# Zeros of the gate cells stored during attention, and twelve modulation dot products computed under the output projection

## The chip, the cores and the metric

One core of one Trainium2 chip runs the whole kernel. The metric is the device time of one execution in microseconds (us), as the median of three. The engines are TensorE (PE in the profile), VectorE (DVE), ScalarE (ACT), GpSimd (POOL) and SyncE (SP), which here only issues DMAs.

## What is computed

A decoder layer on x (512 tokens x 1024) with a conditioning vector c, all in float32:

```
mod = silu(c) @ w_mod + b_mod            # six parts of 1024: shift_m scale_m gate_m shift_f scale_f gate_f
h = rms_norm(x, pre_mix_gain) * (1 + scale_m) + shift_m
y = hybrid_mixer(h)                      # differential attention and gated DeltaNet heads, then y @ w_out
x = x + gate_m * rms_norm(y, post_mix_gain)
h = rms_norm(x, pre_ffn_gain) * (1 + scale_f) + shift_f
y = peer_ffn(h)                          # 8 heads pick 16 of 128^2 experts per token
x = x + gate_f * rms_norm(y, post_ffn_gain)
```

The peer stage doesn't gather expert rows for 384 of the 512 tokens. It multiplies by all experts in 128 tiles and needs a dense array of gate weights in DRAM (`gate_scratch`, 128 x 128 x 384 cells), nearly all zero, into which the picked gates are scattered.

## The kernel before, in words

Each engine's program is written out by hand; semaphores order them, and each engine and each DMA queue works strictly in its own order. Every float32 weight tile (128x1024, 512 KB) is split in two for PE: ACT casts it to `whi`, and DVE or POOL subtracts to get the remainder `wlo`; PE then does three products. Tiles are numbered through the kernel: 0 to 7 (values, z), 8 to 15 (keys and queries of attention), 16 to 27 (DeltaNet's q, k, v), 28 to 35 (`w_out`), 36 to 51 (query), 52 on (experts). Four raw buffers take them from DRAM; `load_raw(n, ...)` on SP waits for remainder n-4.

**Modulation.** `mod` is taken as 48 column tiles of 128x1024, each reduced on DVE against silu(c) in `gate_f` by one instruction, `mod_tile(m)` (L1756, both operands in SBUF), which then counts up `s_modu`. Tiles 0 to 15 give shift_m and scale_m, 16 to 23 gate_m, 24 to 39 shift_f and scale_f, 40 to 47 gate_f (much later). `mod_columns` (L1763 to L1766) turns the sums into the columns `acol` and `bcol`, a few tiny instructions; those of the second half are first used when the second norm is applied, after the output projection (L816 on ACT, L2176 on DVE). SP loads the tiles: of 16 to 39 four before each of the weight tiles 8 to 13. `EARLY` is 32: tiles 24 to 31 run on DVE ahead of attention, 32 to 39 two at a time in its first four steps, with `mod_columns` in the fourth.

**Attention** is run in 18 steps (s = 0 to 17), step s sharing its time with weight tile 10+s on PE: PE multiplies that tile, then does `scores(s)` (L1272), `transposes(s-1)` (L1281) and `values(s-2)` (L1298). ACT casts tile 12+s and takes exponentials, POOL makes the remainders (`lo`, L624), DVE does `biased` (L1891), the modulation tiles, the convolutions from step 6 on and `difference` (L1901 to L1906), on which PE's transposes wait. After it come the decay rows and their exponent in `E` (the buffer `vbeta`), then some 55 us of inverting triangular blocks, and the scan over four chunks (to 307).

**Zeros.** POOL fills `zeros` (8 KB per partition, over attention's keys) after the last scores, L642, and SP stores it 24 times, 1 MB each (L518), after the loads of tiles 28 to 31 and before those of 32 to 35. POOL waits for them (`s_zst`) before it scatters the first gates.

**Output projection** (PE, 307 to 354): tiles 28 to 31 into banks 0 to 3 for all four token blocks (`out_tile`, L1579 to L1581), with `head_transposes` 4 to 7 (L1535) between the first of them, then tiles 32 to 35 block by block into banks 4 to 7 (L1599 to L1601). Around it: ACT casts tiles 30 to 35 (`out_hi`, L1020) and rounds the transposed heads (`o_rounded`, L998); DVE makes their remainders (`o_remainder`, L2101: one operand in PSUM); each `out_tile` waits for two. POOL makes the weight remainders of tiles 30 to 35 (L670), then those of query tiles 36 and 37 (L675). When the first four banks are done, ACT squares them (L1030) and DVE multiplies them by the gate (`y_by_gate`, L2144, the bank is in PSUM). Then per block b: ACT squares the second half, DVE `block_mean` (L2132, L2134), a root on ACT, DVE adds into `xn` (L2166), ACT squares that (L1062) and scales it (L1041). PE transposes the scaled blocks (L1612, L1619), with short dummy products between them (`WARM_QUERY`, L1615), and starts the query projection (L1635) once the norm's columns have been applied.

SP's order here: the loads of tiles 28 to 31, the 24 stores, tiles 32 to 35, x again (four loads, after the heads are normed), query tiles 36 to 39, then the stores of x1.

Of the kernel before, what the change touches and what calls it, by code (L numbers as in the profile page):

```python
# [35 lines left out]
P = 128  # L36
# [46 lines left out]
FIRST_PACED, LAST_PACED = 7, 124  # L83
POOL_DOWN = 9
LAST = 2
EARLY = 32
GDN_ORDER = (4, 5, 6, 7, 0, 1, 2, 3, 8, 9, 10, 11)
WARM = 11
WARM_QUERY = 6
# [10 lines left out]
def build(nc, x, c, mod_tiles, mod_bias_col, gain_cols, in_tiles,  # L100
# [6 lines left out]
    with ExitStack() as ctx:  # L107
# [87 lines left out]
        QKT = at("QKT", [P, NB, 512], F32)  # L195
        wT = at("wT", [P, NB, 512], F32)
        egT = at("egT", [P, NB, 512], F32, cursor[0] - NB * 512 * 4)
        carried = vbeta[:, 0, :]
        E = vbeta
        v_copy = {10: state, 11: vnew}  # L200
# [74 lines left out]
        qTs = at("qTs", [P, 2, SEQ], F32)  # L275
        hfl2 = at("hfl2", [P, 4, SEQ], F32)
        modf = at("modf", [P, 8, D], F32, phase + 32 * 1024)
        zeros = at("zeros", [P, NB * SEQ], F32, kq)
        cursor[0] = phase + 64 * 1024
        whi4 = at("whi4", [P, WSLOT, D], F32R)  # L280
        wlo4 = at("wlo4", [P, WSLOT, D], F32R)
# [178 lines left out]
        def mod_slot(m):  # L460

            if m < 16:
                t = modr[:, m % 8, :]
            elif m < 40:
                t = modx[:, m % 4, :] if m % 8 < 4 else modr[:, m % 4, :]
            else:
                t = modf[:, m % 8, :]
            return t, s_modl[m % 8], 16 * (m // 8 + 1)
# [8 lines left out]
        def _(sp):  # L477
# [7 lines left out]
            def load_mod(m):  # L485
                if m == 16:
                    sp.wait_ge(s_xT, KD)
                if 8 <= m < 40:
                    sp.wait_ge(s_modu, m - 7)
                dst, landed, _ = mod_slot(m)  # L490
                dq(dst, mod_tiles[m]).then_inc(landed, 16)

# [10 lines left out]
            for dst, src in [(mrow[:, 0:48], conv_col),  # L503
                             (hgain, head_gain_cols),
                             (alog4, a_log.partition_broadcast(P)),
                             (dt4, dt_bias.partition_broadcast(P)),
                             (lam_in, lambdas.partition_broadcast(P))]:
                dq(dst, src).then_inc(s_hc, 16)
            for n in range(T_KQ, T_OUT):
                for m in range(4 * n - 16, min(4 * n - 12, 40)):  # L510
                    load_mod(m)
                load_raw(n, in_tiles[n if n < T_GDN else T_GDN + GDN_ORDER[n - T_GDN]])
            for n in range(4):
                load_raw(T_OUT + n, out_tiles[n])
            gate_cells = gate_flat[0:CELLS].rearrange("(p q) -> p q", p=P)
            sp.wait_ge(s_zm, 1)
            for q in range(TD * P // (NB * SEQ)):
                dq(gate_cells[:, q * NB * SEQ:(q + 1) * NB * SEQ], zeros[:]).then_inc(s_zst, 16)  # L518
            for n in range(4, 8):
                load_raw(T_OUT + n, out_tiles[n])  # L520

            sp.wait_ge(s_on, NB)
            for b in range(NB):
                dq(xn[:, b, :], x[b]).then_inc(s_xr, 16)
            for n in range(4):
                load_raw(T_QUERY + n, query_tiles[n])
            for b in range(NB):
# [75 lines left out]
        def _(pool):  # L603
# [33 lines left out]
            lo(T_KQ + 1, T_KQ + 1)  # L637
            pool.wait_ge(s_lo, SLOT0 + 1)
            lo(SLOT0 + 1, SLOT0 + 1)
            lows(SLOT0 + 2, T_OUT)  # L640
            pool.wait_ge(s_sc, H * NB)
            g.memset(zeros[:], 0.0).then_inc(s_zm, 1)  # L642

            for n in range(4 * NB):
                k, t = divmod(n, NB)
# [21 lines left out]
            for n in range(T_OUT + 2, T_QUERY):  # L667
# [2 lines left out]
                g.tensor_tensor(l[:], raw[:, n % RAW, :].rearrange("p (a n) -> p a n", a=2),  # L670
                                h[:].bitcast(F32), ALU.subtract).then_inc(s_lo, 1)

            for n in range(2):
                pool.wait_ge(s_hi, T_QUERY + n + 1)
                g.tensor_tensor(wlo4[:, 2 + n, :], raw[:, (T_QUERY + n) % RAW, :],  # L675
                                whi4[:, 2 + n, :].bitcast(F32), ALU.subtract).then_inc(s_lo, 1)
# [9 lines left out]
            expert_rows = expert_tiles.rearrange("n p d -> (n p) d")  # L686

            gate_cells = gate_flat.unsqueeze(1)
            pool.wait_ge(s_zst, 16 * TD * P // (NB * SEQ))
            for b in range(NG):  # L690
                for k in range(PICKS):
                    if k % MGROUP == 0:
# [42 lines left out]
        def _(act):  # L735
# [135 lines left out]
            for s in range(T_OUT - SLOT0):  # L871
                if s < H * NB:
                    hi(SLOT0 + s + 2)
                if SLOT0 + s < T_GDN:
                    kq_copy(SLOT0 + s)
                if s == H * NB:
                    act.wait_ge(s_oa, SUMS_AT + 1)
                    sc.activation(k_sums, k_sums, ACT.Ln, bias=eps_t).then_inc(s_l2r, 1)
                    act.wait_ge(s_l2, 1)
                    sc.activation(q_sums, bank[2][:, 0:16], ACT.Ln, bias=eps_t).then_inc(s_l2r, 1)  # L880
                if s < H * NB:
                    exps(s)
                if 1 <= s <= H * NB:
                    copy_t(s - 1)
                if s == H * NB:
                    act.wait_ge(s_used, T_OUT - 1)
                    sc.copy(v_copy[10][:], bank[T_OUT % 2][:]).then_inc(s_vc, 1)
                    hi(T_OUT)
                if s in (10, 14):
                    g = (s - 10) // 4  # L890
                    c0 = GDN_ORDER[4 * g]
                    act.wait_ge(s_conv, 4 * g + 4)
                    sc.activation(qkvT[:, c0:c0 + 4, :], qkvT[:, c0:c0 + 4, :],
                                  ACT.Silu).then_inc(s_silu, 1)
                    if g == 0:
                        act.wait_ge(s_modu, 40)
                if s in (11, 14):
                    g = (s - 11) // 3
                    c0 = GDN_ORDER[4 * g]
                    act.wait_ge(s_silu, g + 1)  # L900
                    for n in range(c0, c0 + 4):
                        sc.activation(l2r[:, n, :], qkvT[:, n, :], ACT.Square).then_inc(s_sq, 1)
# [816 lines left out]
        def _(dve):  # L1719
# [127 lines left out]
            dve.wait_ge(s_baT, 1)  # L1847
            v.tensor_copy(baT[:], bank[2][0:8, :]).then_inc(s_bac, 1)
            for m in range(24, EARLY):
                if m == 29:  # L1850
                    dve.wait_ge(s_lo, SLOT0)
                    weight_low(SLOT0)
                mod_tile(m)
            dve.wait_ge(s_lame, 1)
            tt(lam[:, 2:3], lam[:, 0:1], lam[:, 1:2], ALU.subtract)
            v.drain()
# [83 lines left out]
            for s in range(T_OUT - SLOT0):  # L1940
                if 3 <= s <= H * NB + 1:
                    attn_out(s - 3)
                if s < H * NB:
                    biased(s)
                if s == H * NB:
                    k_columns()
                for m in range(EARLY + 2 * s, min(EARLY + 2 * s + 2, 40)):
                    mod_tile(m)
                if EARLY + 2 * s == 38:
                    mod_columns(1, 0, KD)  # L1950
                if T_GDN <= SLOT0 + s < T_OUT - 2:
                    conv(SLOT0 + s - T_GDN)
                if s < H * NB:
                    difference(s)

            for t in range(NB):
                dve.wait_ge(s_row, t + 1)
                decay_args(E, t, ROW_BANK[t], M_NOT_AFTER).then_inc(s_du[0], 1)
# [163 lines left out]
            mean_squares(NB - 1)  # L2123
            gated_heads(NB - 1)
            normed_heads(NB - 1)
            for k in range(4, KD):
                o_remainder(k)

            def block_mean(b):  # L2130
# [362 lines left out]
```

## Time and profile before

| | |
|---|---|
| median of three runs | 1694.61 us (1694.39 to 1695.78) |
| the profiled execution | 1693.73 us |
| its span, first to last instruction | 1691.9 us |
| PE busy | 1675.7 us, 99% |
| DVE busy | 1200.0 us, 71% |
| ACT busy | 691.0 us, 41% |
| POOL busy | 910.8 us, 54% |
| mean granted TensorE clock | 0.998 |
| modulation tiles 0 to 39 on DVE (L1756) | 57.5 us in 40 instructions |

All starts are counted in us from the first instruction. "Busy" of PE is modelled from pipelined matmuls and says little by itself; what counts is where PE has idle time in front of an instruction, which a timeline gives in brackets with the engine that ended it.
### The profile page before, as it was taken

Reading aid. Unit: us, or ns where it says so; the run is one execution under the profiler, and the core shown is the slowest. Engines: PE = TensorE matmul, PEld = TensorE weight load, DVE = VectorE, ACT = ScalarE, POOL = GpSimd, SP = SyncE. Lnnn points to the kernel's source line nnn. Section 1 sums busy time; section 2 is a strip of 40 time slices with the busy share of each in tenths; the row PEclk is TensorE's granted clock in tenths of the full one; section 3 lists DMA queues with packets and bytes.
Section 4 is the critical chain, followed back from the end, with each engine's and each line's share of the span. In section 5 each row is a group of like instructions: output and inputs, shape, how many; then the busy total and the mean of one; then the engine's idle time right before and its main releaser. Section 6 shows DMA issues by size and latency. Waiting matters only on the chain.

```text
span 1691.9 us, 25803 instructions
## 1 busy us (share of the span) xinstructions
PE 1675.7 (99%) x8018; PEld 1389.1 (82%) x8018; DVE 1200.0 (71%) x2991; ACT 691.0 (41%) x1049; POOL 910.8 (54%) x730
## 2 busy tenths in 40 slices
PE   9999999999999999999999999999999999999998
PEld 7777888878888888888888888888888888888886
DVE  8877576446697887777777732224888888888886
ACT  6445564553342244444344434423333333333333
POOL 0133213413357666667666776664676776777630
PEclk9999999999999999999999999999999999999999
DMA  9932393332246444444444444449999999999994
GB/s 372 334 121 72 126 417 133 122 127 75 88 143 241 142 147 150 143 143 143 149 140 141 149 149 149 138 142 351 332 367 378 342 390 350 374 373 349 390 337 154
DMA packets 149221, 375.69 MB, mean 222 GB/s; under 512 B 32033, under 2 KB 64929, under 8 KB 145954
## 3 DMA queue, kind: packets, MB, share of 16 engines
q1 hardware_dynamic: 114338, 307.52, 50.8%
q0 software_dynamic: 34816, 67.41, 11.1%
q8 instruction: 25, 0.41, 0.1%
q14 instruction: 42, 0.34, 0.1%
HBM read 311.73 MB, written 63.11 MB: 222 GB/s over the span
## 4 chain that ended last, share of the span: by engine, by line
PE 95%; DVE 2%; DMA 1%; ACT 1%; DVEq 0%; SPq 0%; issue 0%; ACTq 0%
PE bank L1184 17%; PE bank L1185 17%; PE bank L1186 17%; PE bank L1684 10%; PE bank L1686 10%; PE bank L1688 10%; PE bank L1445 1%; PE bank L1629 1%; DMA g_in<-gate_scratch 1%; PE bank L1272 1%; PE bank L1427 1%; PE bank L1298 1%; PE bank L1461 1%; PE bank L1226 0%; PE bank L1581 0%; PE bank L1601 0%
## 5 line engine op out<-in xcount | busy, mean ns | idle before, releaser
L701 POOL DMA_INDIRECT gate_scratch<-merged,idx_cell x384 | 429.9, 1120 | 213.8 <-issue 106.6
L1184 PE MATMUL bank<-act_hi,whi 128*128 128x512 f32 x1296 | 508.3, 392 | 0.0
L1186 PE MATMUL bank<-act_hi,wlo 128*128 128x512 f32 x1296 | 505.1, 390 | 0.0
L1185 PE MATMUL bank<-act_lo,whi 128*128 128x512 f32 x1296 | 505.1, 390 | 0.0
L2189 DVE TENSOR_TENSOR wlo<-raw,whi 128x1024 fp32r<-128x1024 f32 x247 | 302.0, 1223 | 225.5 <-ACT whi L1092 224.0
L1684 PE MATMUL bank<-whi,chi 128*128 128x512 f32 x768 | 298.8, 389 | 0.7 <-DVE clo L2366 0.7
L1686 PE MATMUL bank<-wlo,chi 128*128 128x512 f32 x768 | 298.8, 389 | 0.0
L1688 PE MATMUL bank<-whi,clo 128*128 128x512 f32 x768 | 298.8, 389 | 0.0
L1186 PEld LDWEIGHTS bank<-act_hi,wlo 128*128 128x128 f32 x1296 | 243.6, 188 | 50.9
L1184 PEld LDWEIGHTS bank<-act_hi,whi 128*128 128x128 f32 x1296 | 243.8, 188 | 49.7
L1185 PEld LDWEIGHTS bank<-act_lo,whi 128*128 128x128 f32 x1296 | 243.8, 188 | 49.4
L1098 ACT ACTIVATE aout<-bank 128x512 f32<-128x512 f32 x128 | 76.6, 599 | 370.2 <-PE bank L1186 357.7
L719 POOL DMA_INDIRECT rows<-in_expert_tiles,idx_row x128 | 171.4, 1339 | 104.5 <-DVE ysp L2381 78.9
L624 POOL TENSOR_TENSOR wlo<-raw,whi 128x1024 fp32r<-128x1024 f32 x35 | 84.9, 2429 | 232.2 <-ACT whi L748 232.2
L1129 ACT CAST chi<-coef 128x384 fp32r<-128x384 f32 x128 | 65.6, 513 | 323.0 <-PE bank L1688 179.2
L710 POOL DMA_INDIRECT asp<-act_scratch,idx_act x128 | 160.9, 1257 | 56.4 <-issue 38.4
L2381 DVE SCALAR_TENSOR_TENSOR ysp<-rows,csp,ysp 128x1024 f32<-128x1024 f32 x127 | 163.2, 1285 | 12.1 <-issue 0.4
L1684 PEld LDWEIGHTS bank<-whi,chi 128*128 128x128 f32 x768 | 144.2, 188 | 31.0 <-issue 1.1
L1688 PEld LDWEIGHTS bank<-whi,clo 128*128 128x128 f32 x768 | 144.2, 188 | 29.8
L1686 PEld LDWEIGHTS bank<-wlo,chi 128*128 128x128 f32 x768 | 144.2, 188 | 29.8
L1092 ACT CAST whi<-raw 128x1024 fp32r<-128x1024 f32 x128 | 133.4, 1042 | 1.0 <-DMA raw<-in_expert_tiles 0.7
L1143 ACT CAST whi<-raw 128x1024 fp32r<-128x1024 f32 x125 | 131.2, 1049 | 0.0
(392 smaller groups left out, 1840.5 us busy)
## 6 DMA issues: line engine op xcount, KB each, us to landing
raw<-in_expert_tiles SPq DMA_DIRECT2D x256, 512.0 KB
act_scratch<-aout SPq DMA_DIRECT2D x128, 256.0 KB, 2.1
gate_scratch<-zeros SPq DMA_DIRECT2D x24, 1024.0 KB, 22.2
a_in<-act_scratch SPq DMA_DIRECT2D x128, 192.0 KB, 7.0
g_in<-gate_scratch SPq DMA_DIRECT2D x128, 192.0 KB
modr<-in_mod_tiles SPq DMA_DIRECT2D x28, 512.0 KB, 10.7
raw<-in_in_tiles SPq DMA_DIRECT2D x28, 512.0 KB
raw<-in_query_tiles SPq DMA_DIRECT2D x16, 512.0 KB
```

The source lines that it names most:

```text
L701: g.indirect_dma_start(out=gate_cells, out_offset=bass.IndirectOffsetOnAxis(ap=idx_cell[:, b, k:k + 1], axis=0), in_=merged[:, b, k:k + 1] ...
L710: g.indirect_dma_start(out=asp[:, k:k + 1], out_offset=None, in_=act_cells, in_offset=bass.IndirectOffsetOnAxis(ap=idx_act[:, k:k + 1], ax ...
L719: g.indirect_dma_start(out=rows[:, k % ROWS, :], out_offset=None, in_=expert_rows, in_offset=bass.IndirectOffsetOnAxis(ap=idx_row[:, k:k + ...
L1092: sc.copy(whi4[:, n % WSLOT, :], raw[:, n % RAW, :]).then_inc(s_hi, 1)
L1184: mm(out_bank[:], whi[:, slot, w], act_hi[:, k, :], start=(k == 0), stop=False)
L1185: mm(out_bank[:], whi[:, slot, w], act_lo[:, k, :], start=False, stop=False)
L1186: last = mm(out_bank[:], wlo[:, slot, w], act_hi[:, k, :], start=False, stop=(k == KD - 1))
L1684: mm(o, chi[:, j % WSLOT, a], whi4[:, j % WSLOT, w], start=start, stop=False, skip_group_check=True)
L1686: mm(o, chi[:, j % WSLOT, a], wlo4[:, j % WSLOT, w], start=False, stop=False, skip_group_check=True)
L1688: return mm(o, clo[:, j % WSLOT, a], whi4[:, j % WSLOT, w], start=False, stop=stop, skip_group_check=True)
L2189: tt(wlo4[:, n % WSLOT, :], raw[:, n % RAW, :], whi4[:, n % WSLOT, :].bitcast(F32), ALU.subtract).then_inc(s_lo, 1)
L2381: stt(out=ysp[:], in0=rows[:, k % ROWS, :], scalar=c, in1=ysp[:], op0=ALU.mult, op1=ALU.add).then_inc(s_axpy, 1)
```

## The change

`EARLY` goes from 32 to 28: modulation tiles 24 to 27 stay ahead of attention, none runs in it, and 28 to 39 with `mod_columns` run on DVE after the heads are normed, between and behind o remainders 4 to 7. Their buffers are six slots of 128x1024 in `Tm`, `PM` and `va`, which are free then; SP loads six of them after the u/w products (`s_uw`), between out tiles 33 and 34, and the other six after x, ahead of the query tiles, each when the tile six before it is used. POOL waits for tile 35 (`s_modu` 36) before it writes the remainders of the query tiles, which lie over `Tm`.

`zeros` becomes the buffer `vbeta`, filled by POOL between the remainders of weight tiles 11 and 12. SP stores it twice after each of the loads of weight tiles 13 to 24. DVE waits for all 24 before it writes `E` there.

```diff
-EARLY = 32
+EARLY = 28
+FILLS = 24
+FILL_FROM = 13
+LATE_SLOTS = 6
...
+        zeros = vbeta
+        late_mods = [ap[:, a:a + 2, :].rearrange("p a n -> p (a n)")
+                     for ap in (Tm, PM, va) for a in (0, 2)]
...
-        zeros = at("zeros", [P, NB * SEQ], F32, kq)
...
+            elif m < EARLY:
+                t = modx[:, m % 4, :] if m % 8 < 4 else modr[:, m % 4, :]
             elif m < 40:
-                t = modx[:, m % 4, :] if m % 8 < 4 else modr[:, m % 4, :]
+                t = late_mods[(m - EARLY) % LATE_SLOTS]
...
-                if 8 <= m < 40:
+                if 8 <= m < EARLY:
                     sp.wait_ge(s_modu, m - 7)
+                elif EARLY + LATE_SLOTS <= m < 40:
+                    sp.wait_ge(s_modu, m - LATE_SLOTS + 1)
...
             for n in range(T_KQ, T_OUT):
-                for m in range(4 * n - 16, min(4 * n - 12, 40)):
+                for m in range(4 * n - 16, min(4 * n - 12, EARLY)):
                     load_mod(m)
                 load_raw(n, in_tiles[n if n < T_GDN else T_GDN + GDN_ORDER[n - T_GDN]])
+                if n == FILL_FROM:
+                    sp.wait_ge(s_zm, 1)
+                for q in range(max(2 * (n - FILL_FROM), 0), min(2 * (n - FILL_FROM) + 2, FILLS)):
+                    dq(gate_cells[:, q * NB * SEQ:(q + 1) * NB * SEQ],
+                       zeros[:].rearrange("p t n -> p (t n)")).then_inc(s_zst, 16)
             for n in range(4):
                 load_raw(T_OUT + n, out_tiles[n])
-            gate_cells = gate_flat[0:CELLS].rearrange("(p q) -> p q", p=P)
-            sp.wait_ge(s_zm, 1)
-            for q in range(TD * P // (NB * SEQ)):
-                dq(gate_cells[:, q * NB * SEQ:(q + 1) * NB * SEQ], zeros[:]).then_inc(s_zst, 16)
-            for n in range(4, 8):
-                load_raw(T_OUT + n, out_tiles[n])
+            load_raw(T_OUT + 4, out_tiles[4])
+            load_raw(T_OUT + 5, out_tiles[5])
+            sp.wait_ge(s_uw, NB)
+            for m in range(EARLY, EARLY + LATE_SLOTS):
+                load_mod(m)
+            load_raw(T_OUT + 6, out_tiles[6])
+            load_raw(T_OUT + 7, out_tiles[7])
 
             sp.wait_ge(s_on, NB)
             for b in range(NB):
                 dq(xn[:, b, :], x[b]).then_inc(s_xr, 16)
+            for m in range(EARLY + LATE_SLOTS, 40):
+                load_mod(m)
...
             pool.wait_ge(s_lo, SLOT0 + 1)
             lo(SLOT0 + 1, SLOT0 + 1)
+            pool.wait_ge(s_baT, 1)
+            g.memset(zeros[:], 0.0).then_inc(s_zm, 1)
             lows(SLOT0 + 2, T_OUT)
-            pool.wait_ge(s_sc, H * NB)
-            g.memset(zeros[:], 0.0).then_inc(s_zm, 1)
...
+            pool.wait_ge(s_modu, EARLY + LATE_SLOTS + 2)
             for n in range(2):
                 pool.wait_ge(s_hi, T_QUERY + n + 1)
...
-                        act.wait_ge(s_modu, 40)
+                        act.wait_ge(s_modu, EARLY)
...
             for m in range(24, EARLY):
-                if m == 29:
-                    dve.wait_ge(s_lo, SLOT0)
-                    weight_low(SLOT0)
                 mod_tile(m)
+            dve.wait_ge(s_lo, SLOT0)
+            weight_low(SLOT0)
...
-                for m in range(EARLY + 2 * s, min(EARLY + 2 * s + 2, 40)):
-                    mod_tile(m)
-                if EARLY + 2 * s == 38:
-                    mod_columns(1, 0, KD)
...
+            dve.wait_ge(s_zst, 16 * FILLS)
             for t in range(NB):
                 dve.wait_ge(s_row, t + 1)
                 decay_args(E, t, ROW_BANK[t], M_NOT_AFTER).then_inc(s_du[0], 1)
...
-            for k in range(4, KD):
-                o_remainder(k)
+            mod_tile(28)
+            o_remainder(4)
+            o_remainder(5)
+            for m in range(29, 32):
+                mod_tile(m)
+            o_remainder(6)
+            o_remainder(7)
+            for m in range(32, 40):
+                mod_tile(m)
+            mod_columns(1, 0, KD)
```

## Rows read from the trace of the kernel before

**Rows 1.** The page, part 4: the chain that ended last, by engine.

```profile
PE 95%; DVE 2%; DMA 1%; ACT 1%; DVEq 0%; SPq 0%; issue 0%; ACTq 0%
```

**Rows 2.** Waits of PE, whole run: us in total, times, longest us.

```profile
PE bank L1281 <- DVE pr L1906: 0.8, 2, 0.7
```

**Rows 3.** Timeline of PE, second attention step: start us, us, engine line op out<-in [idle before].

```profile
92.94 0.33 PE L1281 MATMUL bank<-ident,pr 128*128 128x128 f32 x1 [0.68 <-DVE pr L1906]
```

**Rows 4.** Timeline of DVE, modulation tiles before and in attention.

```profile
59.24 3.42 DVE L1756 CUSTOM_DVE_ANT_0 modr<-modr,gate_f 128x1024 f32<-128x1024 f32 x1
...
87.98 2.80 DVE L1756 CUSTOM_DVE_ANT_0 modx<-modx,gate_f 128x1024 f32<-128x1024 f32 x1
...
90.71 1.22 DVE L1756 CUSTOM_DVE_ANT_0 modx<-modx,gate_f 128x1024 f32<-128x1024 f32 x1
```

**Rows 5.** Timeline of DVE, output projection to the last block's mean.

```profile
315.41 0.75 DVE L2101 SCALAR_TENSOR_TENSOR act_lo<-bank,mrow,act_lo 128x512 fp32r<-128x512 f32 x1 [2.12 <-ACT act_lo L998]
...
321.76 0.75 DVE L2101 SCALAR_TENSOR_TENSOR act_lo<-bank,mrow,act_lo 128x512 fp32r<-128x512 f32 x1 [4.08 <-ACT act_lo L998]
...
334.11 2.48 DVE L2144 TENSOR_TENSOR xs<-bank,gate_m 128x512 f32<-128x512 f32 x4 [10.08 <-ACT osq L1030]
338.62 0.62 DVE L2132 TENSOR_TENSOR small<-small 128x1 f32<-128x1 f32 x1 [2.02 <-ACT osq L1030]
...
354.87 0.16 DVE L2132 TENSOR_TENSOR small<-small 128x1 f32<-128x1 f32 x1 [1.59 <-ACT osq L1030]
```

**Rows 6.** Timeline of POOL, output projection.

```profile
313.10 2.43 POOL L670 TENSOR_TENSOR wlo_x<-raw,whi_x 128x1024 fp32r<-128x1024 f32 x1 [11.42 <-ACT whi_x L1020]
...
322.74 2.40 POOL L670 TENSOR_TENSOR wlo<-raw,whi 128x1024 fp32r<-128x1024 f32 x1 [2.49 <-ACT whi L1020]
328.13 2.39 POOL L670 TENSOR_TENSOR wlo_x<-raw,whi_x 128x1024 fp32r<-128x1024 f32 x1 [2.99 <-ACT whi_x L1020]
333.57 2.42 POOL L670 TENSOR_TENSOR wlo_y<-raw,whi_y 128x1024 fp32r<-128x1024 f32 x1 [3.05 <-ACT whi_y L1020]
336.83 4.75 POOL L675 TENSOR_TENSOR wlo<-raw,whi 128x1024 fp32r<-128x1024 f32 x2 [0.85 <-ACT whi L741]
```

**Rows 7.** Timeline of ACT, output projection.

```profile
327.00 1.05 ACT L1020 CAST whi_x<-raw 128x1024 fp32r<-128x1024 f32 x1 [3.75 <-PE bank L1581]
...
343.75 0.58 ACT L1030 ACTIVATE osq<-bank 128x512 f32<-128x512 f32 x1
...
348.71 0.60 ACT L1030 ACTIVATE osq<-bank 128x512 f32<-128x512 f32 x1 [0.59 <-PE bank L1601]
```

**Rows 8.** Timeline of POOL, before and in attention's first steps.

```profile
58.95 2.63 POOL L624 TENSOR_TENSOR wlo<-raw,whi 128x1024 fp32r<-128x1024 f32 x1 [55.95 <-ACT whi L748]
...
80.78 2.40 POOL L624 TENSOR_TENSOR wlo<-raw,whi 128x1024 fp32r<-128x1024 f32 x1 [13.56 <-ACT whi L748]
86.97 2.73 POOL L624 TENSOR_TENSOR wlo<-raw,whi 128x1024 fp32r<-128x1024 f32 x1 [3.79 <-ACT whi L748]
```

**Rows 9.** The tile `zeros`: its stores and its memset.

```profile
L518 SPq DMA_DIRECT2D gate_scratch<-zeros x24: 343/1255/4209, 203.1 to 240.5; - x24
L642 POOL MEMSET zeros<- x1: 1809/1809/1809, 201.3 to 201.3; 128x2048 f32 x1
```

**Rows 10.** Timeline of ACT, the cast of weight tile 14.

```profile
98.86 1.05 ACT L748 CAST whi<-raw 128x1024 fp32r<-128x1024 f32 x1 [4.01 <-PE bank L1186]
```

**Rows 11.** Windows of ten us: us, busy by engine (instructions), PEclk, DMA share, GB/s.

```profile
250.00:260.00 10.00, 10.00 (x93) 8.68 (x91) 7.51 (x14) 4.27 (x10) 4.54 (x6) 1.00 1.01 416
...
270.00:280.00 10.00, 10.00 (x96) 8.62 (x94) 7.09 (x12) 3.68 (x8) 4.05 (x2) 1.00 0.32 107
```

**Rows 12.** Timeline of SP's queue, the first query tiles.

```profile
320.30 16.04 SPq L496 DMA_DIRECT2D raw<-in_query_tiles  x4
```

**Rows 13.** Windows of ten us, as rows 11.

```profile
190.00:200.00 10.00, 10.00 (x43) 7.51 (x43) 4.95 (x13) 8.53 (x13) 2.08 (x2) 0.83 0.16 54
...
350.00:360.00 10.00, 9.31 (x64) 8.17 (x62) 5.38 (x14) 5.85 (x12) 0.00 (x0) 1.00 0.27 107
```

More of the change, by code:

```diff
@@ L508, in _ @@
                 dq(dst, src).then_inc(s_hc, 16)
+            gate_cells = gate_flat[0:CELLS].rearrange("(p q) -> p q", p=P)
             for n in range(T_KQ, T_OUT):
-                for m in range(4 * n - 16, min(4 * n - 12, 40)):
+                for m in range(4 * n - 16, min(4 * n - 12, EARLY)):
                     load_mod(m)
                 load_raw(n, in_tiles[n if n < T_GDN else T_GDN + GDN_ORDER[n - T_GDN]])
+                if n == FILL_FROM:
[3 more added lines that the diff above has]
+                       zeros[:].rearrange("p t n -> p (t n)")).then_inc(s_zst, 16)
             for n in range(4):
                 load_raw(T_OUT + n, out_tiles[n])
-            gate_cells = gate_flat[0:CELLS].rearrange("(p q) -> p q", p=P)
-            sp.wait_ge(s_zm, 1)
-            for q in range(TD * P // (NB * SEQ)):
-                dq(gate_cells[:, q * NB * SEQ:(q + 1) * NB * SEQ], zeros[:]).then_inc(s_zst, 16)
-            for n in range(4, 8):
-                load_raw(T_OUT + n, out_tiles[n])
+            load_raw(T_OUT + 4, out_tiles[4])
[5 more added lines that the diff above has]
+            load_raw(T_OUT + 7, out_tiles[7])
             sp.wait_ge(s_on, NB)
@@ L688, in _ @@
             gate_cells = gate_flat.unsqueeze(1)
-            pool.wait_ge(s_zst, 16 * TD * P // (NB * SEQ))
+            pool.wait_ge(s_zst, 16 * FILLS)
             for b in range(NG):
```

## The prediction

> **What bounds the kernel now.** Read first the chain of work that ended last [rows 1]: 95% of the span is TensorE (PE) matmuls, so only what makes PE wait, or lets it start sooner, can move the time. Second, PE's own waits over the whole run [rows 2]: the only one that the attention stage's VectorE (DVE) work causes is 0.8 us in two pieces. PE's timeline shows the larger, 0.68 us, at 92.94 [rows 3]. Behind it stand two modulation tiles (32 and 33) on DVE, from 87.98 to about 91.9 [rows 4]. Third, the timelines of DVE, GpSimd (POOL) and ScalarE (ACT) in the output projection, from 307 to 355, where the change puts twelve such tiles [rows 5 to 7]. There PE has no gap at all until 354.1; DVE looks nearly free, 10 us idle before 334.11. What the reader is to see is that POOL is not free there, and that DVE and POOL do not run independently.
>
> **One rule read from the trace first.** A modulation tile reads two 128x1024 operands from SBUF. Alone it takes 1.22 us, 1.145 from one start to the next [rows 4]. The tile at 87.98 took 2.80, and POOL's weight remainder at 86.97 took 2.73, so ended at 89.70: the tile ended 1.08 after it [rows 4, 8]. At 59.24 the same: POOL's began at 58.95 while a tile ran, took 2.63 instead of 2.40, and the next tile, issued at 59.24, ended at 62.66, 1.08 after POOL's end. So they exclude each other: whoever waits gets its turn when the running instruction ends, although the other engine has its next one ready. The tiny DVE addition at 338.62 took 0.62 and so ended where the first of POOL's two back-to-back remainders did (336.83 + 2.4), so a held DVE instruction gets in between them [rows 5, 6]. DVE instructions with one operand in PSUM aren't held: the o remainder at 315.41 took 0.75 while POOL ran [rows 5, 6].
>
> The Trainium skill says this as a rule ("SBUF — State Buffer", section "Who interferes with whom"): a DVE instruction with two SBUF inputs and a GpSimd instruction that reads SBUF block each other for the whole instruction. It speaks against this change: by a plain sum of DVE durations the twelve tiles fit, by the rule they don't. The trace agrees with it, with the 2.80 and 3.42 us above.
>
> **Attention, costed.** Removed: tiles 28 to 31 before it (4 x 1.145 = 4.6 us of DVE, under PE's projection tiles, nothing on the path), tiles 32 to 39 and the column step in its first four steps (8 x 1.145 and four holds behind POOL). On the path that is worth PE's 0.8 us and no more, since PE has no other wait for DVE there [rows 2]. Gain 0.8.
>
> Added to the SP queue: 24 stores of zeros, two after each weight tile 13 to 24. Each loads the DMA engines for about 2.5 us (the 24 went out from 203.1 to 240.5 [rows 9] and kept them full to about 264). POOL's memset (1.81 us [rows 9]) now stands between remainders 11 and 12. The first starts at 80.78 and ends at 83.2, the second starts at 86.97 [rows 8], so the memset fits in that pause, to 85.0. SP waits for it with tiles 14 and on queued behind: tile 14 lands after two stores, about 92, tile 15 after four, about 99, tile 16 after six, about 105. ACT wants tile 14 at 98.86 [rows 10] and each next one about 7 us later, 105.8 and 113.2. So 6 us at least are left, and after that 2.5 MB per 7.2 us step is 350 GB/s against the 416 that these engines moved in full stretches [rows 11]. Cost 0; if stores ran at half that rate, PE would wait some 5 us there. DVE's wait for all 24 before the decay rows ends near 160, and those come at 209: 0. The stretch 203 to 264, now free of stores, gains nothing: PE issues 93 instructions in ten us with the DMA engines full and 96 with a third of them busy, in a different mix [rows 11]. ACT's wait for 28 tiles instead of 40 is long over: 0. The six early loads on SP wait for the u/w products (290) and are in by 300: 0.
>
> **Output projection, costed.** The lock has to serve, from 313.1: six weight remainders of 2.4 us (tiles 30 to 35), twelve tiles of 1.1 us and the small column step (0.65, a drain in it), and, if they are ready, the two query remainders (36, 37; 4.75 together) [rows 6]. Walking through it with turns alternating: remainder 30 313.1 to 315.5; tile 28 to 316.6; remainder 31 to 319.0; o remainders 4 and 5 on DVE meanwhile; tile 29 to 320.0; remainder 32 to 322.4; tile 30 to 323.5; remainder 33 to 325.9; tile 31 to 327.0. Only then o remainders 6 and 7, to 328.4 (before: from 321.76). PE's fourth tile wants them when the third ends at 326.9 (ACT's cast at 327.00 starts on that [rows 7]): PE waits 1.4. Remainder 34 to 330.5; tiles 32 to 35 to 335.05 (which also frees POOL's new wait); remainder 35 to 337.5, in time for PE's moved need at 337.9; tile 36 to 338.5; query remainder 36 to 340.9, tile 37 to 342.0, query remainder 37 to 344.4, tiles 38 and 39 and the column step to 347.3.
>
> Loads: tiles 34 to 39 wait for slots (tile m for m-6), the last at 332.8, and the four query tiles on SP are behind them, about 333 instead of 320.3 [rows 12]. ACT wants the first at 337: 0.
>
> Behind the tiles in DVE's order stand the four gate products (2.48 us, PSUM operands), which before began at 334.11 and left 2.0 of slack before the mean of block 0 at 338.62. That mean now comes at 349.8. From there each block takes 4.37 to 4.4 us through ACT and DVE (343.75 to 348.71 less the 0.59 waited for PE [rows 7]), so the mean of block 3 comes at 363.0 instead of 354.87 [rows 5]: 8.1 us. PE's 1.4 lies inside it, since PE's last block then ends at 355.5 and PE has to wait for this chain anyhow. From there to the query projection all is as before.
>
> **TensorE's clock.** PE will have some 16 us (355.5 to 371) with only transposes and short dummy multiplications. The granted clock in thin work: full from 350 to 360, where the present burst of that kind lies, but 0.83 from 190 to 200, that is 3.4 of the ten us at the lower level (1.2 GHz), after 3 us of 128x1 products [rows 13]. Bounds: 0, and 1.7 us (3.4 us at half pace). The new gaps between bursts are about 3 us, nearest to the second, so I take 1.7.
>
> **Sum.** -0.8 + 8.1 + 1.7 = +9.0. The profiled execution took 1693.7 (span 1691.9), which gives 1702.7; the median of the runs is 0.9 higher, 1694.6, so 1703.6.
>
> **Rivals.**
> 1. Forecast, 0.62: the lock fills the output projection. 1701.9 without the clock's drop, 1703.6 with it, 1705.2 if waiting DVE loses to POOL's back-to-back remainders (the same walk then puts block 3's mean 9.7 late).
> 2. Partly, 0.18: the query remainders come after the tiles (ACT's casts late, or POOL's turn lost). The tiles then end at 342.5, the mean of block 3 is 3.3 late, and the run ends at 1697.1, or 1698.8 with the clock. It decides if both query remainders begin after 342.
> 3. No lock to speak of, 0.13: the tiles take 12 x 1.145 + 2.8 of o remainders + 0.65 from 313.3, so end at 330.5, ahead of the gate products. 1693.8, and 1692.1 if the clock's dip at 191 goes too. For it: DVE's 10 us of idle time. Against it: six held tiles in the trace, none that ran through a POOL remainder.
> 4. Faster, over 0.2%, 0.05: PE's steps in the inversion or attention were slowed by stores or by DVE work in a way that its waits don't show. Against it [rows 2, 11].
> 5. The zeros delay weight tiles 14 to 16 in attention, 0.02: +5 on top of any of these.
>
> No-change is within 0.2% (3.4 us, about what a measurement of this kernel can tell): rival 3 and the lower part of rival 2 lie in it. So slower 0.8, same 0.15, faster 0.05. The range, 1696.5 to 1707, leaves out rivals 3 and 4 and takes in the bounds of the clock and of the lock's order.
>
> **What would show it.** In the profile after: tiles of L1756 between 313 and 347 with durations near 2.2 to 3.5 us where POOL's remainders run, and a sum well over 14; POOL remainders of more than 2.4; PE's wait for DVE before the fourth out tile near 1.4; the first gate product near 347, and PE idle some 8 us more between 355 and 372; no wait at 92.9; no raw tile late in 85 to 160. Wrong, if the tiles' mean stays at 1.2 or if the gate products still begin by 337.

## The result, and the profile after

The change made the kernel **slower by 0.31%**: median 1699.23 us of eight runs (1698.40 to 1700.79) against 1694.5 of eight runs of the kernel before on the same chip; ratio 1.0031, 95% interval 1.0020 to 1.0042. The profiled execution took 1700.06 us, 6.4 more than that of before, with a span of 1698.3 against 1691.9. The forecast was 1703.6, in a range of 1696.5 to 1707.0. So the medians moved by 4.7 us where 9.1 was forecast.

PE's waits after the change, whole run (us in total, times, longest us; beside [rows 2]):

```profile
PE bank L1631 <- DVE xn L2189: 3.0, 1, 3.0
PE bank L1631 <- ACT xs L1060: 1.6, 1, 1.6
...
PE bank L1598 <- DVE act_lo L2116: 1.2, 1, 1.2
...
PE bank L1618 <- POOL wlo_y L688: 0.3, 1, 0.3
```

Three of the four lines are new, the second was 0.2 before; the wait for `pr` in attention (0.8) is gone. L1631 is PE's transposes ahead of the query projection, L1598 the fourth out tile, L1618 the out tiles of the second half. So PE now stands still just where DVE carries the moved tiles, and behind them. The chain that ended last says the same in shares (beside [rows 1]):

```profile
PE 93%; DVE 4%; issue 1%; DMA 1%; ACT 1%; DVEq 0%; SPq 0%; POOL 0%; POOLq 0%; ACTq 0%
```

DVE's timeline from the last head's norm to block 3's mean (beside [rows 5]; L1775 is the modulation tile, 28 to 39 in order, L2116 the o remainder, L2167 the gate product, L2155 the block mean):

```profile
311.88 0.17 DVE L2109 RECIPROCAL gsm<-gsm 128x4 f32<-128x4 f32 x1
...
312.74 3.41 DVE L1775 CUSTOM_DVE_ANT_0 Tm<-Tm,gate_f 128x1024 f32<-128x1024 f32 x1
...
316.08 1.40 DVE L2116 SCALAR_TENSOR_TENSOR act_lo<-bank,mrow,act_lo 128x512 fp32r<-128x512 f32 x2
317.40 2.10 DVE L1775 CUSTOM_DVE_ANT_0 Tm<-Tm,gate_f 128x1024 f32<-128x1024 f32 x1
...
319.43 3.40 DVE L1775 CUSTOM_DVE_ANT_0 PM<-PM,gate_f 128x1024 f32<-128x1024 f32 x1
...
327.42 1.21 DVE L1775 CUSTOM_DVE_ANT_0 va<-va,gate_f 128x1024 f32<-128x1024 f32 x1
...
345.93 2.48 DVE L2167 TENSOR_TENSOR xs<-bank,gate_m 128x512 f32<-128x512 f32 x4
348.32 0.15 DVE L2155 TENSOR_TENSOR small<-small 128x1 f32<-128x1 f32 x1
...
361.05 0.16 DVE L2155 TENSOR_TENSOR small<-small 128x1 f32<-128x1 f32 x1 [0.42 <-ACT osq L1049]
```

Beside it POOL's timeline (beside [rows 6]):

```profile
312.63 2.43 POOL L688 TENSOR_TENSOR wlo_x<-raw,whi_x 128x1024 fp32r<-128x1024 f32 x1 [11.42 <-ACT whi_x L1039]
315.03 3.38 POOL L688 TENSOR_TENSOR wlo_y<-raw,whi_y 128x1024 fp32r<-128x1024 f32 x1
...
338.49 5.84 POOL L694 TENSOR_TENSOR wlo<-raw,whi 128x1024 fp32r<-128x1024 f32 x2 [0.84 <-ACT whi L760]
```

Read the first lines of the two together. POOL's remainder runs from 312.63 to about 315.0; the tile, issued at 312.74, ends at 316.15, 1.1 later. POOL's next remainder was issued at 315.03 and takes 3.38: about 1.0 in which the tile still ran, and its own 2.4. Then a tile, then POOL, in turn. The groups of L1775 between 310 and 347 sum it up (busy us, mean ns):

```profile
L1775 DVE CUSTOM_DVE_ANT_0 va<-va,gate_f 128x1024 f32<-128x1024 f32 x4 | 11.3, 2857 | 0.0
L1775 DVE CUSTOM_DVE_ANT_0 PM<-PM,gate_f 128x1024 f32<-128x1024 f32 x4 | 11.3, 2855 | 0.0
L1775 DVE CUSTOM_DVE_ANT_0 Tm<-Tm,gate_f 128x1024 f32<-128x1024 f32 x4 | 7.9, 1982 | 0.0
```

That is 30.5 us for twelve tiles that need 1.14 to 1.22 each: eight were held. DVE, which before idled 10 us ahead of its gate products, now has no idle time there, and the gate products begin at 345.93 instead of 334.11.

**A ruler for the stage.** Executions differ in where this stage begins (309.63 us in e9 to 312.78 in e1, and 318.58 in e6), so I measure the stage inside each execution: from DVE's last `gsm` reciprocal (all heads normed) to PE's first product of the query projection. Before the change, DVE's and PE's timelines:

```profile
312.35 0.17 DVE L2094 RECIPROCAL gsm<-gsm 128x4 f32<-128x4 f32 x1
```

```profile
362.72 0.47 PE L1635 MATMUL bank<-act_hi,whi 128*128 128x512 f32 x1 [1.25 <-DVE act_lo L1778]
```

and after it, on PE:

```profile
327.64 0.47 PE L1598 MATMUL bank<-whi_y,act_lo 128*128 128x512 f32 x1 [1.20 <-DVE act_lo L2116]
...
368.91 0.47 PE L1654 MATMUL bank<-act_hi,whi 128*128 128x512 f32 x1 [1.25 <-DVE act_lo L1797]
```

362.72 - 312.35 = 50.37 before and 368.91 - 311.88 = 57.03 after: the stage is **6.66 us longer**, which is all that was lost: the span grew by 6.4, since the stage began 0.47 earlier, and what follows it took 0.2 longer. By the same ruler, every kernel of the experiments below, one profiled execution of each:

| kernel | stage, us | over before |
|---|---|---|
| before | 50.37 | 0 |
| after | 57.03 | +6.66 |
| e1 zeros only | 50.38 | +0.01 |
| e2 tiles only | 56.83 | +6.46 |
| e3 query remainders after the tiles | 56.91 | +6.54 |
| e4 no SBUF reads on POOL | 50.41 | +0.04 |
| e5 spread in attention | 50.37 | 0.00 |
| e6 the same, with the zeros | 50.39 | +0.02 |
| e7 query remainders after the columns | 53.86 | +3.49 |
| e8 eight late tiles | 50.39 | +0.02 |
| e9 query remainders twice | 61.26 | +10.89 |

Ten-us windows after the change (columns as in [rows 11], beside [rows 13]):

```profile
190.00:200.00 10.00, 10.00 (x43) 7.39 (x42) 5.00 (x14) 8.49 (x12) 2.05 (x2) 0.83 0.17 54
350.00:360.00 10.00, 7.04 (x38) 5.77 (x37) 5.68 (x15) 7.04 (x15) 0.00 (x0) 1.00 0.27 107
360.00:370.00 10.00, 6.43 (x49) 5.36 (x47) 5.80 (x14) 7.18 (x16) 0.00 (x0) 1.00 0.26 105
```

PE is down to 7.04 and 6.43 busy us in ten, and the granted clock stays at full speed: the clock costs nothing. The dip at 190 is as it was in this execution, but it doesn't belong to the kernel. The window of e3, whose code is that of the change up to the output projection:

```profile
190.00:200.00 10.00, 10.00 (x53) 7.80 (x53) 6.49 (x16) 9.91 (x16) 3.21 (x2) 1.00 0.18 54
```

**How the time ahead of the stage divides.** Counted from PE's first weight product (near 19 to 20 us) to the stage's beginning, before and e1 take 293.10 and 293.07 us, the change 292.09, and e2, e3, e4, e5, e7, e8 and e9 all 290.48 to 290.50. The first three have the dip at 190 (0.83 in its window), the seven have not (1.00). So with the dip on both sides the removal of attention's wait is worth 1.0 us, and an execution without the dip is another 1.6 shorter. The change's own profile shows that its absence isn't assured by the new order; how often it comes, one profile per kernel can't tell.

### The profile page after: what moved, and what is told of

Its sections match the earlier page's. It is cut to its first block, busy times and chain, and to the rows that moved or that the text cites. A ratio compares the mean times of both kernels' runs of the same rounds, so it can differ in the third digit from the quotient of the medians.

```text
span 1698.3 us, 25805 instructions
## 1 busy us (share of the span) xinstructions
PE 1677.3 (99%) x8018; PEld 1389.8 (82%) x8018; DVE 1207.3 (71%) x2991; ACT 689.7 (41%) x1049; POOL 919.1 (54%) x730
## 4 chain that ended last, share of the span: by engine, by line
PE 93%; DVE 4%; issue 1%; DMA 1%; ACT 1%; DVEq 0%; SPq 0%; POOL 0%; POOLq 0%; ACTq 0%
PE bank L1203 17%; PE bank L1204 17%; PE bank L1205 17%; PE bank L1703 10%; PE bank L1705 10%; PE bank L1707 10%; PE bank L1464 1%; PE bank L1648 1%; DMA g_in<-gate_scratch 1%; PE bank L1291 1%; DVE va L1775 1%; DVE PM L1775 1%; PE bank L1446 1%; PE bank L1317 1%; PE bank L1480 1%
```

## The experiments

e1 to e4 and e5 to e8 are two sets, each with its own runs of the kernel before, and e9 is a third by itself, so ratios compare across sets and medians only within one. The medians of before are 1692.68, 1694.29 and 1693.01.

### The two halves apart (e1, e2)

e1 is the kernel before with the zeros' part of the diff alone: tiles 32 to 39, their loads and the column step stay as before. Its edit to the kernel before:

```diff
+        zeros = vbeta
...
-        zeros = at("zeros", [P, NB * SEQ], F32, kq)
...
+                if n == FILL_FROM:
+                    sp.wait_ge(s_zm, 1)
+                for q in range(max(2 * (n - FILL_FROM), 0), min(2 * (n - FILL_FROM) + 2, FILLS)):
...
+            dve.wait_ge(s_zst, 16 * FILLS)
```

e2 is the change with the zeros, their memset and the 24 stores put back where they were. Its edit to the change:

```diff
-        zeros = vbeta
+        zeros = at("zeros", [P, NB * SEQ], F32, kq)
...
-                if n == FILL_FROM:
-                    sp.wait_ge(s_zm, 1)
...
+            sp.wait_ge(s_zm, 1)
+            for q in range(FILLS):
+                dq(gate_cells[:, q * NB * SEQ:(q + 1) * NB * SEQ], zeros[:]).then_inc(s_zst, 16)
...
```

> Only the zeros part of the change; the modulation tiles stay as before, in attention. Theory A (in the output projection DVE's twelve tiles and POOL's weight remainders take turns at one lock, and that alone makes the change slower): as before, ratio 1.000 within 0.001, PE's 0.8 us wait at attention's second step still there, no new wait. Theory B (DVE's order is simply too full there, lock or not): the same as A. Theory C (the stores or the changed loads on SP's queue cost the time): 4 to 6 us slower than before, with weight tiles that land late.

> Only the moved modulation tiles; the zeros are made and stored as before. Theories A and B: as slow as the whole change, ratio about 1.003 (4 to 6 us over before), the gate products start near 346 in the profile. Theory C: no slower than before.

e1: 1692.72 us, ratio 1.0000 (0.9991 to 1.0009). e2: 1698.31, ratio 1.0033 (1.0020 to 1.0045). PE's waits in e1 still hold the one of attention, and none for a raw tile or for what the stores could delay:

```profile
PE bank L1285 <- DVE pr L1910: 0.8, 2, 0.7
```

PE's waits in e2 are those of the change:

```profile
PE bank L1629 <- DVE xn L2186: 2.8, 1, 2.8
...
PE bank L1596 <- DVE act_lo L2113: 1.2, 1, 1.2
```

The zeros are free, and the twelve tiles carry the whole loss.

### POOL without reads (e4)

POOL's remainders of tiles 30 to 37 are replaced by two fills each, about as long together (2 x 0.95 us), which write the same buffers and read none. The third product of those tiles is thereby made with zeros: this kernel leaves out that part of the computation, though PE does as many products.

```diff
-                g.tensor_tensor(l[:], raw[:, n % RAW, :].rearrange("p (a n) -> p a n", a=2),
-                                h[:].bitcast(F32), ALU.subtract).then_inc(s_lo, 1)
+                g.memset(l[:].bitcast(F32), 0.0)
+                g.drain()
+                last = g.memset(l[:].bitcast(F32), 0.0)
+                last.then_inc(s_lo, 1)
...
```

> The changed kernel with POOL's remainders of out tiles 30 to 35 and query tiles 36 and 37 left out: instead POOL writes zeros to each of the eight buffers twice (1.8 us each, no operand read), so those tiles' third product is with zeros. POOL stays occupied for most of the time, but reads nothing. Theory A: every modulation tile takes 1.22 us, they end near 330, the gate products start at 333.6 when the banks are done, and the time falls by 6.6 us from the changed kernel's, to about 1 us under before. Theory B: 2 us at most, the tiles still end after the gate products' due time. Theory C: no change.

1691.68 us, ratio 0.9994 (0.9985 to 1.0003), stage +0.04. POOL's and DVE's timelines:

```profile
311.37 0.95 POOL L688 MEMSET wlo_x<- 128x1024 f32 x1 [11.41 <-ACT whi_x L1043]
312.45 0.95 POOL L690 MEMSET wlo_x<- 128x1024 f32 x1
```

```profile
311.49 1.22 DVE L1779 CUSTOM_DVE_ANT_0 Tm<-Tm,gate_f 128x1024 f32<-128x1024 f32 x1
...
326.94 1.23 DVE L1779 CUSTOM_DVE_ANT_0 Tm<-Tm,gate_f 128x1024 f32<-128x1024 f32 x1 [2.28 <-DMA Tm<-in_mod_tiles]
...
335.08 2.48 DVE L2171 TENSOR_TENSOR xs<-bank,gate_m 128x512 f32<-128x512 f32 x4
```

The tile at 311.49 runs beside a fill at its full pace. All twelve take 1.22 or 1.23, eight of them beside a fill. Now their loads set the pace (2.28 us of waiting for tile 34), and it no longer matters. This is the decisive run: the same twelve tiles, in the same place, cost nothing once POOL reads nothing. Not the number of tiles, not their loads, but the exclusion is the price. (A pair of fills is also 0.4 us shorter than the remainder in whose place it stands; the tiles beside a fill show that it isn't this.) The Trainium skill ("SBUF — State Buffer", section "Who interferes with whom") says that a DVE instruction with two SBUF inputs contends with a GpSimd instruction that reads SBUF and "not with one that only writes it"; the trace agrees, 3.41 against 1.22 us.

### The query remainders later (e3, e7) and twice (e9)

The walk put the last tiles and the column step behind POOL's query remainders 36 and 37. All three are edits to the change. e3 lets POOL wait for all 40 tiles first:

```diff
-            pool.wait_ge(s_modu, EARLY + LATE_SLOTS + 2)
+            pool.wait_ge(s_modu, 40)
```

e7 lets it wait for the column step as well:

```diff
-            pool.wait_ge(s_modu, EARLY + LATE_SLOTS + 2)
+            pool.wait_ge(s_cols, 6)
```

e9 makes each of the two remainders twice:

```diff
-                g.tensor_tensor(wlo4[:, 2 + n, :], raw[:, (T_QUERY + n) % RAW, :],
-                                whi4[:, 2 + n, :].bitcast(F32), ALU.subtract).then_inc(s_lo, 1)
+                for again in range(2):
+                    last = g.tensor_tensor(wlo4[:, 2 + n, :], raw[:, (T_QUERY + n) % RAW, :],
+                                           whi4[:, 2 + n, :].bitcast(F32), ALU.subtract)
+                    if again == 0:
+                        g.drain()
+                last.then_inc(s_lo, 1)
```

> The changed kernel, but POOL waits for all 40 modulation tiles, not for 36, before its two remainders of query tiles 36 and 37. Neither has work added or removed. Theory A: the lock is free for the last tiles, so they end 4.7 us earlier, the mean of block 3 comes near 356.3 instead of 361.05 in the profile, and the time falls by 4 to 4.8 us, to about that of before (1694.5). The query remainders then run from about 341 to 346, long before PE needs them. Theory B: DVE's own work is as long as ever, so no change, 1699. Theory C: no change.

> The changed kernel, but POOL waits for the column step that follows modulation tile 39 before its two query remainders. In the run where it waited for the 40 tiles alone, the two remainders began at 339.77 and held the column step's tiny additions, 2.40 and 2.20 us, where the tiles had been held before. Theory A (the lock counts, however small the held instruction): the column step takes 0.6 us, the gate products start near 340.4 instead of 344.5, one held addition into xn costs 1 us, and the mean of block 3 comes 2.8 us earlier than there: 1695 to 1696 against 1698.5. Theory B (DVE's own work is too long): no change, 1698.5.

> The changed kernel, but POOL makes each of the remainders of query tiles 36 and 37 twice, one after the other: 4.8 us more of POOL reading SBUF, and nothing that PE waits for before 369. Theory A (turns at one lock): these four take turns with tile 38, tile 39 and the two additions of the column step, each of which is held for a whole remainder, so the gate products start near 350.3 instead of 345.93 and the time rises by 4.4 us over the changed kernel, to about 1703. Theory B (DVE's own work is too long): no change, 1699.

e3: 1698.52 us, ratio 1.0033 (1.0021 to 1.0045), no gain at all, where I had expected all of it back. The tiles did end sooner, 29.2 us after the reciprocal instead of 33.5. DVE's timeline of e3 shows who took it back:

```profile
338.47 1.22 DVE L1775 CUSTOM_DVE_ANT_0 va<-va,gate_f 128x1024 f32<-128x1024 f32 x1
...
339.79 2.40 DVE L1782 TENSOR_TENSOR bcol<-modcol,modbcol 128x8 f32<-128x8 f32 x1
...
342.35 2.20 DVE L1785 SCALAR_TENSOR_TENSOR acol<-acol,gaincol 128x8 f32<-128x8 f32 x1
```

POOL's two remainders start at 339.77, in the 0.1 us between the end of the last tile and the column step. Two of its three instructions on 128x8 (the first an addition, the last an addition and a multiplication in one), 0.17 us each when alone, are held for a whole remainder each: 2.40 + 2.20. I had moved the collision instead of removing it.

e7: 1696.76 us, ratio 1.0013 (1.0003 to 1.0023), stage +3.49. The column step is free now, and POOL's remainders (from 339.57) meet the next thing, DVE's addition into `xn`. DVE's timeline of e7:

```profile
339.00 0.17 DVE L1782 TENSOR_TENSOR bcol<-modcol,modbcol 128x8 f32<-128x8 f32 x1
...
339.41 2.48 DVE L2167 TENSOR_TENSOR xs<-bank,gate_m 128x512 f32<-128x512 f32 x4
...
342.97 2.45 DVE L2189 SCALAR_TENSOR_TENSOR xn<-xs,small,xn 128x1024 f32<-128x1024 f32 x1
```

The addition takes 2.45 instead of 1.28; block 3's mean comes at 355.75, 46.0 after the reciprocal, against 49.17 in the change and 42.52 before. While the four gate products ran (one operand in PSUM), the first remainder cost nobody anything: 2.48, as ever. The profiled execution of e7 was the slowest of its eleven (1701.63): behind PE's first query product it took 1336.2 us, where that of the change took 1329.4. So its span can't be compared with the others, and its stage can.

e9: 1702.49 us, ratio 1.0052 (1.0039 to 1.0066), stage +10.89, so 4.2 above the change. DVE's timeline of e9:

```profile
339.78 3.40 DVE L1779 CUSTOM_DVE_ANT_0 va<-va,gate_f 128x1024 f32<-128x1024 f32 x1
...
343.28 2.18 DVE L1786 TENSOR_TENSOR bcol<-modcol,modbcol 128x8 f32<-128x8 f32 x1
...
345.62 2.38 DVE L1789 SCALAR_TENSOR_TENSOR acol<-acol,gaincol 128x8 f32<-128x8 f32 x1
```

Doubling the suspected cost cost DVE 2.18 + 2.38 on the column step, less the 0.33 that these two take alone: 4.2, and 4.4 was expected. The theory gives the size as well as the sign.

e9 also shows what the change didn't: here the clock fell. PE's timeline, and two windows as above:

```profile
356.80 0.87 PE L1635 MATMUL bank<-ident,xs 128*128 128x128 f32 x6 [3.35 <-ACT xs L1064]
361.31 1.97 PE L1635 MATMUL bank<-ident,xs 128*128 128x128 f32 x8 [3.63 <-DVE xn L2193]
```

```profile
350.00:360.00 10.00, 4.32 (x22) 3.15 (x20) 6.28 (x20) 5.52 (x15) 0.00 (x0) 0.93 0.26 105
360.00:370.00 10.00, 7.96 (x50) 7.53 (x50) 5.61 (x12) 6.90 (x14) 0.00 (x0) 0.72 0.26 105
```

PE paused 3.35 us, worked 0.87 and paused 3.63; windows of one us show the lower level (1.2 GHz) from about 358.7 to 365.5. The eight transposes took 1.97 us instead of the 1.09 of the change. Yet the stage lost nothing by it: from block 3's mean to PE's first query product there are 7.85 us in e9 (363.04 to 370.89) and 7.86 in the change, because DVE's and ACT's chain sets that end: PE still waits for DVE at the end of it, 0.39 us before the last transposes and 1.25 before the product.

### Fewer tiles late (e8)

e7 with `EARLY` at 32, so that only tiles 32 to 39 run late and none runs in attention.

```diff
-EARLY = 28
+EARLY = 32
...
-            mod_tile(28)
+            mod_tile(32)
...
-            for m in range(29, 32):
+            for m in range(33, 35):
...
```

> The run before, but with tiles 28 to 31 back ahead of attention, where they lay under PE's work; only tiles 32 to 39 run in the output projection. Theory A: the lock has to serve six remainders (14.4 us), eight tiles (8.8) and the columns (0.65) from 312, so it is through by 336, and the gate products are on time. PE's wait in attention stays gone: 0.8 to 0.9 us under before, about 6.5 under the changed kernel. Theory B: DVE's own time falls by 4.6 us, so 4.6 under the changed kernel, still 2 over before.

1692.95 us, ratio 0.9991 (0.9982 to 1.0001), stage +0.02. DVE's timeline of e8:

```profile
332.23 2.41 DVE L1783 TENSOR_TENSOR acol<-modcol,modbcol 128x8 f32<-128x8 f32 x1
...
334.81 2.48 DVE L2168 TENSOR_TENSOR xs<-bank,gate_m 128x512 f32<-128x512 f32 x4
...
338.93 2.45 DVE L2190 SCALAR_TENSOR_TENSOR xn<-xs,small,xn 128x1024 f32<-128x1024 f32 x1
...
353.50 0.16 DVE L2156 TENSOR_TENSOR small<-small 128x1 f32<-128x1 f32 x1 [1.59 <-ACT osq L1049]
```

DVE instructions are still held, but all within the slack: the last mean waits 1.59 for ACT's square of PE's bank, as it did in [rows 5], so PE sets the pace again. Of the versions with the whole change's structure this is the best. Its gain over before, 1.3 us in the medians, is between what attention's wait gives and what it gives together with the absent dip at 190 (1.0 and 2.6 by the profiles), and at the edge of what these runs can tell: the interval just holds 1.

### Tiles spread in attention (e5), and the zeros with that (e6)

What the change did for attention can be had without moving a tile out of it. e5 is the kernel before with one of tiles 32 to 39 per step in steps 0 to 3 and two in steps 4 and 5; tiles 36 to 39 are loaded ahead of weight tiles 16 to 19. e6 is e5 with the zeros' part of the change.

```diff
+SPREAD = (32, 33, 34, 35, 36, 38, 40)
...
+                if 16 <= n < 20:
+                    load_mod(n + 20)
...
-                for m in range(EARLY + 2 * s, min(EARLY + 2 * s + 2, 40)):
+                for m in range(SPREAD[s], SPREAD[s + 1]) if s < 6 else ():
...
```

> The kernel before, zeros as there, but the modulation tiles 32 to 39 spread over more of attention's steps: one in each of steps 0 to 3, two in steps 4 and 5, instead of two in each of steps 0 to 3. Theory A: PE's 0.8 us wait for DVE in attention goes, nothing is added anywhere, so 0.8 us under before: ratio 0.9995, at the edge of what five rounds tell. In the profile no wait of the transposes (L1281 of before), and no longer modulation tiles in the output projection. Theory D (DVE's work in attention slows PE in other ways than by that wait): more than 2 us under before.

> As the run before with the stores of zeros between attention's weight tiles added. Theory A: the same as that run, 0.8 us under before, since the stores were never on the path. Theory C: slower by a few us.

e5: 1692.97 us, ratio 0.9996 (0.9984 to 1.0008): PE's wait for `pr` is gone from the list, and what it brought can't be told from nothing. e6: 1702.26 us, ratio 1.0051 (1.0038 to 1.0065), which I had not expected. Timelines of e6, DVE and then PE:

```profile
116.31 1.56 DVE L1765 CUSTOM_DVE_ANT_0 modx<-modx,gate_f 128x1024 f32<-128x1024 f32 x1 [1.77 <-DMA modx<-in_mod_tiles]
123.74 1.23 DVE L1765 CUSTOM_DVE_ANT_0 modx<-modx,gate_f 128x1024 f32<-128x1024 f32 x1 [2.73 <-DMA modx<-in_mod_tiles]
131.58 1.23 DVE L1765 CUSTOM_DVE_ANT_0 modx<-modx,gate_f 128x1024 f32<-128x1024 f32 x1 [6.60 <-DMA modx<-in_mod_tiles]
```

```profile
134.59 0.69 PE L1290 MATMUL bank<-ident,pr 128*128 128x128 f32 x2 [6.92 <-DVE pr L1915]
```

and two of e6's windows:

```profile
120.00:130.00 10.00, 7.67 (x39) 5.69 (x37) 2.01 (x6) 3.37 (x8) 4.36 (x2) 1.00 1.02 421
130.00:140.00 10.00, 5.42 (x19) 4.48 (x20) 7.73 (x22) 1.56 (x5) 0.37 (x1) 0.66 1.01 421
```

The DMA engines are full (share 1.01 to 1.02, 421 GB/s). The loads of tiles 36 to 39 stand in SP's queue behind 1 MB stores, and the last three come later each time; step 5's `pr` is behind tile 39 on DVE, and PE waits 6.92. The output projection itself is as before (stage +0.02): from PE's first weight product to its beginning there are 299.24 us, 8.75 more than in e5. The rows show 6.92 of it as PE's wait, and a lower clock behind the wait (0.66 in the window). The same stores are free in e1 and in the change, whose modulation tiles were all asked for before the first store. So "zeros cost nothing" holds only while no load with a short date is queued after them.

## Why the prediction was right, point by point

**The mechanism** was the predicted one: DVE's tiles and POOL's remainders exclude each other and take turns. e4 shows it by taking POOL's reads away, e9 by doubling them, e2 that nothing else takes part. Rival 3 (no lock) is refuted by eight held tiles. Rival 2 would have come true if the query remainders had begun late; they began at 338.49, before its bound of 342, and e3 shows that it was priced wrongly as well: it left out that remainders which come late hold the column step. Its 3.3 us is what e7 measured (+3.49), by another way: there the column step ran free and the `xn` addition was held. Rival 5 did not occur: no raw tile came late. Rival 4 did not occur in the change either: beyond attention's wait nothing was gained. The 1.6 us of the absent dip at 190, in seven of the other profiles, are a gain of its kind that rival 3 named; whether the order of attention has a part in it is not shown.

**Attention, -0.8.** The wait at 92.94 is gone. In the profiled pair the heads were normed 0.47 earlier (311.88 against 312.35 us), although PE's first weight product came 0.54 later (19.79 against 19.25), so 1.0 us was gained between, 0.8 of it PE's waits. The size was right for an execution that keeps the dip at 190; the medians of e4, e5 and e8 are 1.0 to 1.3 under before, with 1 in each interval.

**Zeros, 0.** Right: ratio 1.0000 in e1. What the prediction's DMA sum didn't say is its condition, which e6 found.

**PE's wait before the fourth out tile, 1.4.** 1.20 measured, at 327.64. A second small one, 0.3 at L1618, was not forecast: remainder 35 ended at 337.65, which is 338.1 in the walk's time (this execution's stage began 0.47 earlier), 0.6 later than walked.

**End of the tiles and the column step, 347.3.** Measured 345.93, or 346.4 if the 0.47 by which this execution's stage began earlier is added back: 0.9 early. Up to tile 31 the order was the one walked. Then tile 32 got in ahead of remainder 34 and so tile 36 ahead of 35, one tile sooner than in the walk, and behind the second query remainder only tile 39 was left, not 38 and 39.

**Period per block, 4.37 to 4.4.** Measured (361.05 - 348.32) / 3 = 4.24. Three periods make 0.4 less.

**Sum of the lock, +8.1.** 361.05 - 354.87 = 6.2, or 6.65 with the 0.47: 1.4 too much, 0.9 from the tiles' end, 0.4 from the periods, and 0.1 from the gate products to the first mean.

**The clock, +1.7.** This is **the term that failed**. I chose the dip of 190 to 200 as the nearest row, since the gaps between bursts would be about 3 us. The clock stayed at 1.00 in both windows, so its other bound, 0, was the right one: the bursts of transposes and dummy products with gaps of up to 3.0 us kept the clock, as the burst in [rows 13] had. The row that I took was a poor one besides. PE's timeline of before has 1.84 us of 128x1 products there, not 3, and in seven other kernels they passed with the clock at 1.00. And the step from a lower clock to lost time was wrong too: I charged the slower PE to the path in a stretch in which PE waits for DVE and ACT anyhow. In e9 the clock did fall, for some 6.8 us, and the stage lost nothing by it.

Together +9.0 was forecast and +6.4 measured between the profiled executions. Clock and lock account for 3.1 us too much; 0.3 of the 0.8 forecast for attention didn't show in the pair, and 0.2 lies behind the stage. Both errors of size had the same sign, so the forecast was nearly double the 4.7 us that the medians moved; the median lies in the range since its lower end allowed for a clock term of 0. The other 1.7 us of the miss lie in the runs: I added the 0.9 by which the median before stood above its profiled execution, and after the change the median stands 0.8 below it. Such an allowance can have either sign; that the profiled execution of the change had the dip at 190, and other executions may not have, would be one cause, and is not shown.

What stays open: whether attention's 1.0 us is worth anything in a median (e5 and e8 each hold 1 in their interval); what makes the dip at 190 come or stay away; and a tile whose second operand lies in PSUM, which the readings here say would not be held, was not tried.

## What to carry to other kernels

Idle time on DVE is no room for a DVE instruction with two SBUF inputs while POOL reads SBUF: count the two engines' instructions as one queue and walk it in turns, with every small instruction of that kind behind it counted as long as the POOL instruction that it meets. A POOL job moved to make room must be moved past the last such DVE instruction on the path, or under those with an operand in PSUM. And bulk stores on a queue are free only if no load with a date is queued after them.

## What the runs showed of the hardware that I had not expected

- Instructions on 128x8, 0.17 us alone, took 2.40 and 2.20 us while POOL subtracted 128x1024 tiles (e3), and 2.18, 2.38 and 2.41 in e9 and e8: the hold goes by POOL's instruction, not by the size of DVE's.
- POOL's fills (0.95 us for 128x1024) never held a tile: in e4 eight tiles ran beside a fill, at 1.22 or 1.23 us like the other four.
- Thin work did not lower the clock in the change (1.00 with PE 6.43 us busy in ten, in gaps of up to 3.0 us) and did in e9 (0.93 and 0.72, with pauses of 3.35 and 3.63 us and 0.87 of transposes between), where it cost no time. A single pause of 6.92 us in e6 went with 0.66 in its window.
- The same stretch of work near 190 us ran with the clock at 0.83 in three profiles and at 1.00 in seven, with 1.6 us between the change, which had the lower clock, and e3, which hadn't.
- With the DMA engines full at 421 GB/s, DVE waited 1.77, 2.73 and 6.60 us for three 512 KB loads in a row, queued among 1 MB stores.
